# Unread identity products put into TensorE's waits at the expert stages and two norms, and one weight split moved into a norm

## The reference

```
h = layer_norm(h + moe(h))            # twice, ends the first stack
y = rmsnorm(h, norm_mix[0])           # opens the second stack
q, k, v, gate, f = split(y @ fox_w_in)
```

## Time and profile before

| what | value |
|---|---|
| median of 3 runs | 2878.37 us |
| the profiled execution | 2877.56 us |
| its span | 2875.8 us |
| granted TensorE clock, mean | 0.96 |
| PE busy | 2661.9 us (93%) |
| VectorE busy | 1961.3 us (68%) |
| ScalarE busy | 1502.2 us (52%) |
| longest engine on the chain of waits | PE, 77% |

### The profile page before, as it was taken

One profiled execution on the slowest core, in us unless ns is written; L12 is line 12 of the kernel. 1 busy time (PEld: TensorE's weight loads), 2 busy tenths in 40 slices (PEclk: granted clock), 3 DMA queues, 4 the chain that ended last, 5 costly groups with the idle time before them and its releaser, 6 DMA issues.

```text
span 2875.8 us, 55106 instructions
## 1 busy us (share of the span) xinstructions
PE 2661.9 (93%) x21144; PEld 2424.4 (84%) x21144; DVE 1961.3 (68%) x3477; ACT 1502.2 (52%) x2540; POOL 136.1 (5%) x165
## 2 busy tenths in 40 slices
PE   6988889997897999889899998999998899998999
PEld 4845579996866999779699988999888799997999
DVE  2167479996466999764667774677866577766677
ACT  3257368884455888653543454434742443446433
POOL 1010011100000111000000020000010000000000
PEclk8999889998897999989899999999989999999999
DMA  8281179998424999854055542455440155542553
GB/s 301 89 307 60 64 259 372 367 365 298 147 89 143 358 358 359 304 157 148 19 172 174 166 128 92 162 175 176 151 148 1 59 169 174 164 138 74 164 187 118
DMA packets 286158, 528.98 MB, mean 184 GB/s; under 512 B 14288, under 2 KB 207104, under 8 KB 285328
## 3 DMA queue, kind: packets, MB, share of 16 engines
q1 hardware_dynamic: 273312, 499.77, 50.7%
q0 software_dynamic: 9216, 12.61, 1.3%
q10 hardware_dynamic: 3440, 13.98, 1.3%
HBM read 526.21 MB, written 21.06 MB: 190 GB/s over the span
## 4 chain that ended last, share of the span: by engine, by line
PE 77%; DVE 6%; ACT 5%; issue 3%; DMA 1%; ACTq 0%; PEld 0%; PEldq 0%; DVEq 0%; POOLq 0%
PE ps L2365 17%; PE ps L2933 6%; PE ps L2934 6%; PE ps L2935 6%; PE ps L1982 4%; PE ps L1984 4%; PE ps L1983 4%; PE ps L2953 3%; PE ps L2955 3%; PE ps L2954 3%; PE ps L2018 2%; PE ps L2019 2%; PE ps L2020 2%; PE ps L565 2%; PE ps L962 1%
## 5 line engine op out<-in xcount | busy, mean ns | idle before, releaser
L2365 PE MATMUL ps<-H_part,W_hi 128*128 128x272 f32 (+2 forms) x2160 | 490.6, 305 | 25.5 <-DVE H_part L2269 12.7
L2159 DVE TENSOR_TENSOR W_lo<-ring,W_hi 128x1024 fp32r<-128x1024 f32 x384 | 452.6, 1221 | 45.5 <-ACT W_hi L2080 44.4
L2982 ACT ACTIVATE W_hi<-ring 128x1024 fp32r<-128x1024 f32 x264 | 263.1, 1049 | 294.5 <-PE ps L2955 185.9
L2933 PE MATMUL ps<-room_part,W_hi 128*128 128x272 f32 (+1 forms) x1408 | 404.6, 287 | 5.0 <-DVE room_part L2269 5.0
L2080 ACT ACTIVATE W_hi<-ring 128x1024 fp32r<-128x1024 f32 x384 | 384.8, 1052 | 39.0 <-PE ps L1984 18.1
L2934 PE MATMUL ps<-room_part,W_hi 128*128 128x272 f32 (+1 forms) x1408 | 403.5, 287 | 0.0
L2935 PE MATMUL ps<-room_part,W_lo 128*128 128x272 f32 (+1 forms) x1408 | 402.8, 286 | 0.0
L2365 PEld LDWEIGHTS ps<-H_part,W_hi 128*128 128x128 f32 x2160 | 361.5, 192 | 45.8 <-issue 30.0
L2365 PE MATMUL ps<-H_part,W_lo 128*128 128x272 f32 (+2 forms) x1216 | 359.6, 296 | 0.0
L3022 DVE TENSOR_TENSOR W_lo<-ring,W_hi 128x1024 fp32r<-128x1024 f32 x264 | 313.9, 1218 | 10.4 <-ACT W_hi L2982 9.4
L2338 DVE TENSOR_TENSOR W_lo<-ring,W_hi 128x1024 fp32r<-128x1024 f32 x186 | 224.3, 1246 | 120.7 <-ACT W_hi L2330 120.2
(11 more groups left out here) (521 smaller groups left out, 5479.0 us busy)
## 6 DMA issues: line engine op xcount, KB each, us to landing
ring<-in_w_down SPq DMA_DIRECT2D x108, 1024.0 KB, 6.3
ring<-in_w_gate_up SPq DMA_DIRECT2D x88, 1024.0 KB, 5.1
ring<-in_w_gate SPq DMA_DIRECT2D x64, 1024.0 KB, 7.7
ring<-in_w_up SPq DMA_DIRECT2D x64, 1024.0 KB, 7.5
ring<-in_w_mod SPq DMA_DIRECT2D x48, 1024.0 KB, 6.5
ring<-in_fox_w_in SPq DMA_DIRECT2D x32, 1024.0 KB, 5.7
ring<-in_gdn_w_in SPq DMA_DIRECT2D x16, 1024.0 KB, 5.5
ring<-in_gla_w_in SPq DMA_DIRECT2D x12, 1024.0 KB, 5.2
```

Source lines behind the costliest of these rows:

```text
L2159: dve.tensor_tensor(lo, c.ring[:, (self.g0 + p) % SLOTS, W], hi.bitcast(F32), ALU.subtract)\
L2365: mm = pe.matmul(self.out(i), a, b, start=(k == 0 and n_part == 0), stop=(k == KC - 1 and n_part == 2))
L2933: pe.matmul(out, wh[:, k, M], hi, start=(k == 0), stop=False)
L2982: act.activation(self.slot_parts(p)[0][:, C], c.ring[:, g % SLOTS, C], ACT.Copy).then_inc(c.hi_done, 1)
```

## The change

A method `turn_over` multiplies the identity by itself n times into a PSUM bank that nobody reads then. It stands at five places: 40 times before rows(0,0) and 12 times before up G 0 at the opening of each expert stage, 40 times before the outputs are turned at its end, 14 times at the end of the first norm behind an expert stage and 24 times at the end of the second. For the second stack's first projection the split of slot 0 moves into the norm ahead of it (high half behind the root, low half behind the scaled chunks), the split of slot 1 moves behind the chunks, and the eight squares move behind the eight high halves.

```diff
--- before.py
+++ after.py
@@ -282,6 +282,11 @@
         at = view.offset - self.room[:].offset
         n = view.shape[2]
         return [self.room_part[:, at + k * n + T.start:at + k * n + T.stop] for k in range(KC)]
+
+    def turn_over(self, pe, bank, n, at=0):
+
+        for j in range(n):
+            pe.matmul(self.ps[:, bank, at:at + P], self.s("ident"), self.s("ident"), start=True, stop=True)
 
     def mod(self, layer, part, k, stream):
         c = layer * 48 + part * 8 + k
@@ -1262,6 +1267,8 @@
         self.spread(pe, self.ROOTS, self.root).then_inc(self.tensor_done, self.pe.mark("root"))
         if self.mods:
             self.mods.tensor(pe, 0, 1)
+        if self.project:
+            c.turn_over(pe, self.MEANS, 14 if self.mods else 24)
 
     def tail_scalar(self, act):
         c, t = self.c, slice(self.t0, self.t0 + self.tn)
@@ -2033,8 +2040,10 @@
                 rows(n // 2 + 2, 1, i)
             down(n, i)
 
+        c.turn_over(pe, 3, 40)
         rows(0, 0)
         rows(0, 1)
+        c.turn_over(pe, 3, 12)
         up("G", 0)
         rows(1, 0)
         up("U", 0)
@@ -2047,6 +2056,7 @@
         for n in range(N - 4, N):
             step(n, last=(n == N - 1))
         self.mods.tensor(pe, 0, 1)
+        c.turn_over(pe, 2, 40)
         for t in range(self.nt):
             pe.wait_ge(self.picks_added, t + 1)
             if t >= 2:
@@ -2255,12 +2265,20 @@
 
     def split_scalar(self, act):
         c = self.c
+
+        def square(k):
+            act.activation(self.sq[k], c.X[:, k, self.T], ACT.Square).then_inc(self.scalar_done, self.act.mark("sq", k))
+
         for k in range(KC):
             if self.ready:
                 self.ready(act, k)
             act.activation(self.parts[0][k], c.X[:, k, self.T], ACT.Copy, scale=self.gain[:, k:k + 1])\
                .then_inc(self.scalar_done, self.act.mark("hi", k))
-            act.activation(self.sq[k], c.X[:, k, self.T], ACT.Square).then_inc(self.scalar_done, self.act.mark("sq", k))
+            if self.ready:
+                square(k)
+        if not self.ready:
+            for k in range(KC):
+                square(k)
 
     def split_vector(self, dve):
         for k in range(KC):
@@ -2503,12 +2521,15 @@
             self.beside_tensor(pe, i)
 
     def scalar_early(self, act):
-        self.upper(act, 0)
-        self.upper(act, 1)
+        if self.behind:
+            self.upper(act, 0)
+            self.upper(act, 1)
 
     def scalar(self, act):
         c = self.c
         self.split_scalar(act)
+        if not self.behind:
+            self.upper(act, 1)
         self.sums_scalar(act)
         self.upper(act, 2)
         self.root_scalar(act)
@@ -2527,8 +2548,6 @@
             self.beside_scalar(act, i)
 
     def vector(self, dve):
-        if not self.behind:
-            self.lower(dve, 0)
         self.split_vector(dve)
         self.lower(dve, 1)
         self.lower(dve, 2)
@@ -4099,7 +4118,9 @@
     norm = OutNorm(c, OT, m["OT_parts"], [columns(d["w_out_odd"], s * WIDE) for s in range(4)], 1, [(1, CTX)], (1, 3), attention)
     yield norm
     behind = yield from experts(c, norm, 1, CTX, SEQ, 44)
-    yield LayerNorm(c, 1, [(1, CTX)], None, behind, shift_to=META)
+    norm = LayerNorm(c, 1, [(1, CTX)], None, behind, shift_to=META)
+    yield norm
+    return norm
 
 
 def experts(c, behind, layer, t0, tn, first):
@@ -4283,11 +4304,13 @@
     yield AddProject(c, m["OT"], [chunks[2].spread(h) for h in range(8)], [columns(d["gdn_w_out"], s * WIDE) for s in range(4)], 0)
 
 
-def second_stack(c):
+def second_stack(c, norm):
     behind = None
     for i, mixer in enumerate((lambda b: fox(c, 0, 0, b), lambda b: gla(c, 1, b), lambda b: gdn(c, 2, b),
                                lambda b: fox(c, 1, 3, b, META))):
-        for stage in mixer(behind):
+        for n, stage in enumerate(mixer(behind)):
+            if i == 0 and n == 0:
+                norm.project = stage
             yield stage
         behind = swiglu(c, i, stage, META if i == 3 else 0)
         yield behind
@@ -4298,7 +4321,11 @@
 
     with ExitStack() as ctx:
         core = Core(nc, ctx, dram, values)
-        stages = list(first_stack(core)) + list(second_stack(core))
+        def both_stacks():
+            norm = yield from first_stack(core)
+            yield from second_stack(core, norm)
+
+        stages = list(both_stacks())
         if limit:
             stages = stages[:limit]
         for n, stage in enumerate(stages):
```

## The result

The changed kernel took 2896.14 us, median of five runs (2891.07 to 2897.57), against 2878.37 us for the kernel before (2873.39 to 2882.68; its three runs known ahead of the change and two more, which leave the median where it was). The ratio is 1.0062 with a 95% interval of 1.005 to 1.0074: slower by 14 to 21 us, outside the stated range. The profiled execution took 2891.87 us at a span of 2890.0, against 2877.56 at 2875.8 before: +14.3 where +6.0 was forecast. The mean granted clock rose from 0.960 to 0.968, and the kernel became slower all the same.

A forecast was written before the change was run, and what follows sets the result against it. TensorE and DMA were taken as saturated inside expert stages, with cold clock only between them. Openings +8.3, ends 0, first norm -0.8, second -1.5 gave +6.0 on 2877.56: 2883.6 us, range 2872 to 2892.

The forecast's parts named there:

- the openings: Expert openings: batches of 40 and 12 end G 0 4.5 and 3.8 us later, together +8.3, bounds +4.1 to +10.5.
- Rival (b): Openings: a long cold stretch, batch 12.5 us, G 0 10.5 us late; 2888 us in all, chance 0.27.
- The delay is passed on in full: Behind G 0 in the expert stages: TensorE and DMA are saturated, so the whole +8.3 us reaches the total.
- Size and clock of a product: Identity products: two instructions each, 0.118 us warm and 0.22 cold apiece; 40 take 9.4 us warm, 11.5 from cold.
- Rival (a): Openings: the first batches are hidden, as if a product were one instruction; 2871.5 us, chance 0.14.
- (c): Openings: clock does not rise under identity products, each opening some 16 us later; about 2913 us, chance 0.03.
- Stage ends: Expert ends, batch of 40: hidden in stage one, transposes 3 us late in stage two; 0, bounds -0.8 and +1.0.
- Norms: First norm (14 products) -0.8 us; second norm (24) with the moved split -1.5, its batch last to finish.
- Rule (d): All four cold windows: all cold time pays, half of 102 us won; 2827 us, chance 0.03.

The follow-up runs named there:

- open_only: The kernel before with only the two opening batches, 40 and 12, in each expert stage; 2891.29 us against 2875.26, ratio 1.0055.
- jump_40_12: The kernel before with TensorE's untaken dense form emptied and both opening batches, 40 and 12; 2886.45 us in one run against 2875.24.
- after: The changed kernel itself, with all batches and the moved split, against the kernel before; 2896.14 us against 2878.37, ratio 1.0062.
- fit: The changed kernel with 0 and 6 products at the openings, none at stage ends, 14 in first norm, none in second; 2872.28 us against 2876.19, ratio 0.999.
- split_only: The kernel before with only the moved split of the second stack's first weights, no identity products; 2877.75 us, ratio 1.0003.
- open_0_6: The changed kernel without the opening 40 and with 6 in place of the 12; 2871.85 us, ratio 0.9988.
- no_open: The changed kernel without the two opening batches, 40 and 12; 2876.99 us, ratio 1.0009.

## Why the prediction was wrong

**The step that failed** is the first sentence on the openings: "TensorE passes the stage wait together with ScalarE and must load the same flag, so its batch starts at about 372.5, a little before ScalarE's first instruction." It starts 3.82 us behind it (4.19 in `open_only`), and 3.14 us in the second stage (4.45). Counted from the 0.3 us ahead that was assumed, that is 4.1 and 3.4 us, 7.5 together; the two openings missed by 4.3 and 3.0 us, 7.3 together (+15.6 where +8.3 was forecast), and the whole profile by 8.3 (+14.3 against +6.0); the last 1.0 is what the other rows of the table leave, pieces of either sign. In `open_only` the lateness and the miss of the openings are both 9.2 us. In `jump_40_12`, where TensorE does arrive with ScalarE, the same edit cost 7.9 us against the recorded 8.3; in the kernels with the long dense form it cost 15.6 (`after`) and 17.5 (`open_only`). The sign of the terms and the rest of their working were right; the start was not, and with it their size.

The warning stood in the earlier trace rows. L1995 had `[6.75 <-issue]`, idle time that no semaphore ended. I read it as a free gap of 4 us ahead of the rows, and it was the engine arriving. VectorE's L2159 had a releaser by name, ScalarE's W_hi, but ScalarE had written the first of its four parts about 1 us after 372.85 and VectorE came at 376.49: a releaser done long before the start says the same thing. The bounds on this term (+4.1 to +10.5) varied the rate and the clock and held the start fixed, so the range was too narrow where it mattered. Rival (b), slower with openings 10.5 us late in all, named the right place and the right sign; its mechanism, a longer cold stretch, was not what happened: the batches took 12.0 and 11.4 us, against 11.5 forecast and 12.5 in the rival, which is 0.4 us in both together.

**The delay is passed on in full: right.** From the end of G 0 to the last output copy (the second L2105, before the last scatter) the kernels took 291.6 to 291.8 us, and to the last turn L429, in all thirteen kernels, 295.2 to 295.3. Late rows, late gathers and a warm or cold opening change nothing in it.

**Size and clock of a product: right.** 40 products are 80 instructions in 9.18 us warm (9.4) and 11.1 to 12.1 us from cold, 11.65 in the mean of eight (11.5); 12 are 24 in 2.84 (2.8). Rival (a) is refuted by the x80, (c) by the warm rows behind the batch.

**Stage ends: right in kind.** Hidden in stage one, 2.6 us late and given back in stage two. The +2.3 us of stage one were not forecast. About 1 us of them may be the batch's, the rest is not explained: the interval scatters by 2.7 us over the kernels that have no batch there.

**Norms: right in sign and place, the first partly by luck.** First -0.8 as forecast, but the batch took 3.4 us and not 5.0: the clock had not fallen as the prediction took it to have. In `fit` the same 28 instructions did take 5.00. In the second the batch does take the split's place as the last to drain (+0.25 for +0.2), and product 1 comes 1.2 us earlier (1.5). What the prediction did not draw from its own bounds is that the split is better off without the batch: 2.8 us in `split_only`.

**Rule (d), the one that the prediction quotes for the change: refuted here.** The mean clock rose by 0.008, and the time by 14.3 us; the best that products gave with the forms in their old order (`fit` and `open_0_6`, both with the split) was 3 to 4 us, not 51. TensorE waits in those windows, and a wait is not shortened by a faster clock.

## What to carry to other kernels

Before an idle stretch is filled, mark its start: one instruction that waits for nothing, at the head of the code, shows when the engine truly arrives. Idle time put down to "issue" before the first instruction of a branch form may be the branch itself: here emptying the form that is jumped over took it away. The jump belongs where the engine waits anyway. A product put into an in-order queue delays every real one behind it, so it is sized to the wait and not to the clock: 0 and 6 gained some 3 us where 40 and 12 lost 15.

## What was not expected

- Jumping over a long form costs the engine 3 to 4 us and more. At the head of the gathered form TensorE came 4.02 and 3.26 us behind ScalarE, and 0.05 and 0.16 us ahead of it with the body emptied. At the end of a form the same jump stood with 6.51 us on the chain. VectorE showed it too, 3.6 us against 1.09.
- The cold stretches move rather than vanish. With the batch at the first stage end the granted clock was down from 702.8 to 709.6 instead of from 685.3 to 695.5, with 5 us of real work in it instead of 3.3. Further on, between 778 and 800 us, the granted clock was 0.77 in the kernel before and 0.92 in `no_open`; the same 32 instructions took 6.06 us of the chain in the one and 3.66 in the other. Pieces of some 3 us thus differ between kernels at places that no edit touches. They are the reason that a difference of 2 us in one trace is not laid on an edit here.
